# Mixture-of-experts items taken in pairs, with one fp32r gather for two items, and buffers laid out at multiples of 64 bytes

## What is computed

```python
def swiglu(x, w_gate, w_up, w_down):
    return (jax.nn.silu(x @ w_gate) * (x @ w_up)) @ w_down

def moe_swiglu(x, router_w, w_gate, w_up, w_down):      # N_EXPERTS 8, TOP_K 2, D_FF_EXPERT 3584
    logits = (x @ router_w).astype(jnp.float32)
    top_v, top_i = lax.top_k(logits, TOP_K)
    gates = jax.nn.softmax(top_v, axis=-1)
    combine = jnp.sum(jax.nn.one_hot(top_i, N_EXPERTS) * gates[..., None], axis=-2)
    y = jnp.zeros_like(x)
    for e in range(N_EXPERTS):
        y = y + combine[..., e:e + 1] * swiglu(x, w_gate[e], w_up[e], w_down[e])
    return y
```

## Time and profile before

| | us |
|---|---|
| median of 3 runs | 2152.03 (2149.94 to 2154.01) |
| the profiled execution, its own time | 2157.44 |
| its span, first to last instruction | 2154.8, granted TensorE clock 0.974 of full |
| attention, mixers, dense layer, router | 0 to about 1140 |
| items 0 to 7 and the last norm | about 1140 to 2154.8 |
| busy: PE, DVE, ACT | 2088.3 (97%), 1510.5 (70%), 1006.0 (47%) |

### The profile page before, as it was taken

How to read it: one execution, slowest core, us unless ns; L and a number is a source line. 1 busy time by engine, 2 the same in 40 slices (tenths; PEclk the granted TensorE clock), 3 DMA queues, 4 the chain that set the end, 5 groups by cost and what they waited for, 6 DMA issues and landing times.

```text
span 2154.8 us, 28044 instructions
## 1 busy us (share of the span) xinstructions
PE 2088.3 (97%) x10596; PEld 1665.9 (77%) x10596; DVE 1510.5 (70%) x1837; ACT 1006.0 (47%) x1082; POOL 50.9 (2%) x56
## 2 busy tenths in 40 slices
PE   7999999999998999999889999999999999999996
PEld 4786677756876799888747888888888888888885
DVE  4565434554597445438848888898888889888887
ACT  1121312122133334313236777777777777677674
POOL 0000000000011000000200000000000000000000
PEclk9998999999999999999988999999999999999999
DMA  9844043611621265452127999999999999999990
GB/s 356 279 140 159 30 146 99 226 43 38 217 79 40 92 202 196 172 183 81 44 107 291 395 355 368 347 355 372 330 374 337 367 346 355 376 327 375 333 368 20
DMA packets 238710, 502.18 MB, mean 233 GB/s; under 512 B 11275, under 2 KB 53027, under 8 KB 238627
## 3 DMA queue, kind: packets, MB, share of 16 engines
q1 hardware_dynamic: 238626, 501.03, 65.0%
HBM read 499.96 MB, written 1.05 MB: 233 GB/s over the span
## 4 chain that ended last, share of the span: by engine, by line
PE 89%; DVE 7%; ACT 2%; issue 1%; DMA 0%; SPq 0%; DVEq 0%; ACTq 0%
PE bank L1506 12%; PE bank L1489 9%; PE bank L1491 9%; PE bank L1490 9%; PE bank L757 6%; PE bank L1196 6%; PE bank L989 3%; PE bank L1064 3%; PE bank L765 3%; PE bank L1166 3%; PE bank L1433 3%; PE bank L1172 2%; PE bank L1404 2%; PE bank L1403 2%; PE bank L1402 2%; PE bank L1368 2%
## 5 line engine op out<-in xcount | busy, mean ns | idle before, releaser
L2650 DVE TENSOR_TENSOR ring_r<-ring,his 128x2048 fp32r<-128x2048 f32 x240 | 548.7, 2290 | 77.9 <-ACT his L1619 77.2
L1619 ACT ACTIVATE his<-ring 128x2048 fp32r<-128x2048 f32 x240 | 460.2, 1918 | 127.5 <-PE bank L1491 74.7
L1489 PE MATMUL bank<-his,xe_hi 128*128 128x512 f32 x896 | 354.1, 395 | 0.2 <-DVE ring_r L2650 0.2
L1491 PE MATMUL bank<-his,xe_lo 128*128 128x512 f32 x896 | 349.5, 390 | 0.0
L1490 PE MATMUL bank<-ring_r,xe_hi 128*128 128x512 f32 x704 | 274.2, 389 | 0.0
L2650 DVE TENSOR_TENSOR more_raw_r<-more_raw,his 128x2048 fp32r<-128x2048 f32 x96 | 219.7, 2290 | 27.5 <-ACT his L1619 27.4
L1619 ACT ACTIVATE his<-more_raw 128x2048 fp32r<-128x2048 f32 x96 | 184.2, 1919 | 54.6 <-PE bank L1506 29.1
L1489 PEld LDWEIGHTS bank<-his,xe_hi 128*128 128x128 f32 x896 | 168.2, 188 | 37.0 <-DVE ring_r L2650 3.3
L1491 PEld LDWEIGHTS bank<-his,xe_lo 128*128 128x128 f32 x896 | 168.2, 188 | 35.9
L1490 PEld LDWEIGHTS bank<-ring_r,xe_hi 128*128 128x128 f32 x704 | 132.3, 188 | 26.7
L1196 PE MATMUL bank<-uT,ring 128*128 128x256 f32 (+1 forms) x768 | 149.1, 356 | 0.0
(11 more groups left out here) (439 smaller groups left out, 3093.4 us busy)
## 6 DMA issues: line engine op xcount, KB each, us to landing
ring<-in_moe_w_gate_dram SPq DMA_DIRECT2D x96, 1024.0 KB, 5.2
ring<-in_moe_w_up_dram SPq DMA_DIRECT2D x80, 1024.0 KB, 5.3
ring<-in_moe_w_down_dram SPq DMA_DIRECT2D x64, 1024.0 KB, 4.9
more_raw<-in_moe_w_down_dram SPq DMA_DIRECT2D x48, 1024.0 KB, 5.0
ring<-in_w_in_dram SPq DMA_DIRECT2D x16, 2048.0 KB, 11.4
more_raw<-in_moe_w_up_dram SPq DMA_DIRECT2D x32, 1024.0 KB, 5.2
ring<-in_w_ada_dram SPq DMA_DIRECT2D x12, 2048.0 KB, 10.8
ring<-in_w_out_dram SPq DMA_DIRECT2D x8, 2048.0 KB, 9.6
```

The lines of the kernel that those rows point to most:

```text
L1489: mm(bank[b][:, :], xe_hi[:, k, :], hi[:, kk, :], start=(k == 0), stop=False)
L1491: last = mm(bank[b][:, :], xe_lo[:, k, :], hi[:, kk, :], start=False, stop=(k == KD - 1))
L1619: return go(out, in_, ACT.Copy, scale=scale)
L2650: tt(piece_lo(s), piece_raw(s), piece_hi(s).bitcast(fp32), ALU.subtract).then_inc(S("lo_ready"), 1)
```

## The change

Items are taken two at a time. The loop runs over pairs (`Fori(0, more) as m`, `more` is 3 here), its body holds the 14 chunks of items n = 2m and 2m + 1 (a = 0, 1), and an expert list of odd length is filled up with an empty item. x is split once into fp32r x_hi (ACT, two copies [128, 1024]) and x_lo (DVE, two subtractions, written over x); so total = ALPHA * x is formed before the router instead of after the first chunks. `pick` holds two items' places, 256 columns. A gather for a pair is 4 parts f of (4 matmuls from x_hi into bank 5, 4 from x_lo into bank 4), 256 columns each, fp32r; ACT copies all high parts and the odd low parts, DVE the even low parts. In the chunk j == 5 of the second item of a pair the parts stand between the down pieces and the first gate pieces. In the first item's chunk j == 5 nothing is gathered. The last norm's weights are loaded at the end, since they share memory with xe_lo. Buffers whose size is not a multiple of 64 bytes get a 32-byte filler behind them.

```diff
@@ memory
         def sb(name, shape, dtype=fp32):
-            return place[0].enter_context(nc.sbuf_tensor(name, shape, dtype))
+            made = place[0].enter_context(nc.sbuf_tensor(name, shape, dtype))
+            if name not in ("lnst", "lnmv") and 0 < math.prod(shape[1:]) * 4 % LINE <= LINE // 2:
+                place[0].enter_context(nc.sbuf_tensor(f"{name}_fill", [P, LINE // 8], fp32))
+            return made
@@ PE
-            def gather(half):
+            def gather(m, f, lo, b):
-                for f in range(4):
+                if f and not lo:
+                    pe.wait_ge(S("xe_hi_ready"), m * 4 + f)
+                elif f:
+                    pe.wait_ge(S("xe_lo_even" if f % 2 else "xe_lo_odd"), m * 2 + (f + 1) // 2)
+                src = x_lo if lo else x_hi
+                for kk in range(2):
+                    k = 2 * f + kk
                     for i in range(NT):
-                        last = mm(bank[5 - half][:, f * P:(f + 1) * P], x[:, i, (4 * half + f) * P:(4 * half + f + 1) * P],
-                                  pick[:, i, :], start=(i == 0), stop=(i == NT - 1))
+                        last = mm(bank[b][:, kk * 2 * P:(kk + 1) * 2 * P], src[:, i, k * P:(k + 1) * P], pick[:, i, :],
+                                  start=(i == 0), stop=(i == NT - 1))
...
+            def first_up(n, a, m, s0, b):
                 for half in range(2):
+                    if half:
+                        gather_both(m, 3)
+                    pe.wait_ge(S("xe_hi_ready"), m * 4 + (2 * half + 2))
+                    pe.wait_ge(S("xe_lo_even"), m * 2 + (half + 1))
+                    pe.wait_ge(S("xe_lo_odd"), m * 2 + (half + 1))
+                    up_piece(n, a, s0 + half, half, b)
...
                 if j == 5:
                     turn_hidden(g - 1)
+                if j == 5 and a == 1:
                     pe.wait_ge(S("picks_copied"), n + 1)
-                    pe.wait_ge(S("picked"), n + 2)
-                    gather(0)
+                    pe.wait_ge(S("picked"), m + 2)
+                    gather(m + 1, 0, False, 5)
                     pe.wait_ge(S("he_ready"), g)
-                    gather(1)
+                    gather(m + 1, 0, True, 4)
+                    down_piece(n, s0)
+                    gather_both(m + 1, 1)
+                    down_piece(n, s0 + 1)
+                    gather_both(m + 1, 2)
+                    first_up(n, to, m + 1, s0 + 2, b)
+                    s0 += 2
+                elif j == 5:
                     down_pieces(n, g - 1, s0)
                     s0 += 2
-                if j == 5:
-                    pe.wait_ge(S("xe_ready"), n * 2 + 4)
-                up_pieces(n, s0, b)
+                    up_pieces(n, to, s0, b)
@@ ACT
+                def gathered_hi(m, f, b):
+                    act.wait_ge(S("gathered_hi"), m * 4 + (f + 1))
+                    copy(xe_hi[:, :, 2 * f:2 * f + 2, :], bank[b][:, :].rearrange("p (k a s) -> p a k s", k=2, a=2))\
+                        .then_inc(S("xe_hi_ready"), 1)
+                    if f % 2:
+                        act.wait_ge(S("gathered_lo"), m * 4 + (f + 1))
+                        copy(xe_lo[:, :, 2 * f:2 * f + 2, :], bank[b - 1][:, :].rearrange("p (k a s) -> p a k s", k=2, a=2))\
+                            .then_inc(S("xe_lo_odd"), 1)
...
                         if j == 5 and r == 4:
                             copy_out(n)
+                        if j == 5 and a == 1 and r in (1, 2, 3, 4):
+                            gathered_hi(m + 1, r - 1, 5)
@@ DVE, experts(), ahead of the router's logits
+                for i in range(NT):
+                    for c in range(2):
+                        ts(total[:, i, cs], x[:, i, cs], ALPHA, None, ALU.mult).then_inc(S("acc_added"), 1)
+                for i in range(NT):
+                    dve.wait_ge(S("x_hi_ready"), i + 1)
+                    dve.wait_ge(S("acc_added"), 2 * i + 2)
+                    tt(x_lo[:, i, :], x[:, i, :], x_hi[:, i, :].bitcast(fp32), ALU.subtract).then_inc(S("x_lo_ready"), 1)
...
-                gathered_lo(0, [0])
-                combine()
-                gathered_lo(0, [1])
-                chunk(0, -2)
+                for f in (0, 2):
+                    gathered_lo(0, f, 4 + 2 * (f % 2))
+                chunk(0, 0, -2)
+                combine()
                 list_items()
```

More of the change, by code:

```diff
@@ L61 @@
 KE = D_FE // P
+LINE = 64
 RING = 5
@@ L136, in constants @@
     later["level0"] = lv[:, 0].T.copy()
+    later["tri_le"] = (row <= col).astype(np.float32)
+    later["tri_lt"] = (row < col).astype(np.float32)
+    later["iota"] = np.broadcast_to(r[None, :], (P, P)).astype(np.float32)
+    parts["fill"] = np.zeros((P, -sum(v.shape[1] for v in parts.values()) % 64), np.float32)
     at = {}
@@ new lines, in gather_both, with down_piece @@
+            def gather_both(m, f):
+                gather(m, f, False, 5)
+                gather(m, f, True, 4)
+            def down_piece(n, s):
+                half, q = piece_of(s)[3], piece_of(s)[2]
+                pe.wait_ge(S("lo_ready"), n * NPIECE + (s + 1))
+                hi, lo = piece_hi(s), piece_lo(s)
+                for kk in range(2):
+                    k = 2 * half + kk
+                    for a, w in ((he_hi, hi), (he_hi, lo), (he_lo, hi)):
+                        for c in range(2):
+                            last = mm(bank[6 + c][:, :], a[:, k, :], w[:, kk, 512 * c:512 * c + 512],
+                                      start=(q == 0 and k == 0 and a is he_hi and w is hi),
+                                      stop=(q == NQ - 1 and k == 3 and a is he_lo))
+                last.then_inc(S("piece_used"), 1)
@@ L1494, in down_pieces @@
             def down_pieces(n, g, s0):
                 pe.wait_ge(S("he_ready"), g + 1)
[L1497 to L1504, removed]
-                            for c in range(2):
-                                last = mm(bank[6 + c][:, :], a[:, k, :], w[:, kk, 512 * c:512 * c + 512],
-                                          start=(q == 0 and k == 0 and a is he_hi and w is hi),
-                                          stop=(q == NQ - 1 and k == 3 and a is he_lo))
-                    last.then_inc(S("piece_used"), 1)
+                down_piece(n, s0)
@@ L2679, in experts @@
                 for i in range(NT):
[L2680 removed]
+                    for a in range(2):
+                        last = ts(pick[:, i, a * P:(a + 1) * P], C("iota"), places[:, i, a:a + 1], None, ALU.is_equal)
                 last.then_inc(S("first_pick"), 1)
```

243 lines of the change are left out of this document (137 added, 106 removed).

## The result

The changed kernel takes 2181.18 us (median of 4 runs, 2177.92 to 2183.24), the kernel before 2153.02 (4 runs, 2149.94 to 2155.51): a ratio of 1.0124, 95% interval 1.011 to 1.0139. It is slower by 28 us between the medians (27 by the ratio), where 8.7 were forecast with a range up to 2168. The profiled execution took 2177.92 us, its span is 2176.1, against 2157.44 and 2154.8.

The account below looks back on a forecast made before the run. PE was taken to bound the kernel. First items −6.0, second items +7.5, prologue +5.5 and clock +1.7 summed to +8.7 us: 2166.1 on the profiled execution, 2160.7 on the median, range 2148 to 2168.

Parts of the forecast that it names:

- alignment: Term for the addresses of buffers that PE streams in the items: already at multiples of 64, taken as 0.
- (d): Rival: alignment pays over the first 1140 us, making the kernel faster; 2138 us at 2%; chance .08.
- Loop bookkeeping halves, on engines that wait for PE: Term for the expert loop's bookkeeping, listed among the rest at nothing.
- First items: End of each pair's first item: gather gone, down pieces earlier, PE idle 2.0 us; 4 × −1.5 = −6.0 us.
- the 0.3 that was given back for a late VectorE: In first items, 0.3 us off the −1.81 gain, for VectorE catching up behind ye_lo on the next chunk's low half.
- Second items: End of a pair's second item, three in the loop: new PE waits around the gather parts; 3 × 2.5 = +7.5 us.
- the wait at the second gate piece: In second items, PE waits 1.1 us there because ScalarE's copy_out delays the copies of gather part 3.
- Prologue: Router to first expert matmul and piece 4's low half: +3.3 and some 2.2 us of waiting; sum +5.5 us.
- the six operations: VectorE ahead of the first logits: four of total, two subtractions, 3.9 us; less 2.11 idle, logits copy 1.9 us later.
- Clock: PE's clock falls behind one of four new two-microsecond gaps in first items: +1.7 us, bounds 0 and 6.8.
- One sign of being wrong: A first 1120 us that changes by over 2 us would show the prediction wrong.
- the 15.3 us of gather work: PE work saved in the items: seven gathers of 3.83 us become three of 3.8.

Follow-up runs that it names:

- e1: The kernel before with the 32-byte fillers alone; 2160.1 us against 2155.01, ratio 1.0028.
- e2: The changed kernel without the 32-byte fillers; 2180.5 us, ratio 1.0125 against the kernel before.
- e8: The kernel before with PE's loop body two items long, work and addresses unchanged; 2162.49 us, ratio 1.004.
- e5: The changed kernel with 192 more bytes ahead of the experts' buffers, all seven alike modulo 256; 2170.17 us, ratio 1.0074 against the kernel before.
- e9: e5 with four edits of order (he_lo earlier, gather part 3 ahead of copy-out, x_lo and combine moved); 2166.35 us, ratio 1.0059 against the kernel before.
- e3: The changed kernel with 64 more bytes ahead of the experts' buffers; 2179.03 us.
- e10: e9 with the last chunk of a pair's first item in the usual order and its copy-out one chunk later; 2159.24 us, ratio 1.0026 against the kernel before.
- e7: The kernel before with 64 more bytes between his and xe_hi; 2177.05 us (one run).

## Why the prediction was wrong

**The step that failed is the one on alignment**: "The buffers that PE streams in the items (ring, his, xe, he) lie at multiples of 64 already ... I take 0." It asked which buffers the fillers bring to a multiple of 64, and overlooked that they move the others, which were alike modulo 256, apart. The two equal rows it rested on the earlier trace rows are fp32 matmuls of 128 columns at 275 ns, a form that says nothing of 512-column fp32r ones. The term was 0 and measured +17 us in the changed kernel. The fillers are not its only source: alone they cost the kernel before 7.9 us in the items (e1), and without them the changed kernel is as slow (e2), since its other buffers, xe_lo among them, had moved as well. The prediction looked at no address of the changed kernel. The rival drawn from the same edit, (d), had the other sign.

**The second missing term is the fetch.** "Loop bookkeeping halves, on engines that wait for PE" looked at the count of jumps, not at the length of the body. It measured +7.6 us for two jumps; e8 shows it alone, +7.3 between the medians. The trace of before could have told: no instruction packet in its loop, one every 25 us outside.

*First items*: right in place, a little too small. 1.90 us idle for 2.0 forecast, and a gain of 1.76 each where −1.5 stood: the 0.3 that was given back for a late VectorE did not come. *Second items*: right in place and size, +2.6 for +2.5. In e5, where matmuls have their old spacing, two items take 253.4 us from down pieces to down pieces, 4.8 more than before; less the jump's 3.8 that is 1.0 a pair, and 2.5 − 1.5 = 1.0 was forecast. The reason that I gave for the wait at the second gate piece (ScalarE in the copy-out) was wrong: e9 took the copy-out away from there and the wait stayed. *Prologue*: right within a microsecond, 3.1 + 1.8 for 3.3 + 2.2 (the six operations less the idle time are 1.8 us by the rows, where 1.9 was written). *Clock*: the kind was right, two falls where one was forecast; the other profiles of pairs with those gaps (e2, e3, e5, e9) have two, one, none and none behind them. One fall was a guess between none and four, and it could have come out either way. By the Trainium skill's rule (TensorE: Matmul & The Clock Gate, Why this matters for your kernels) there should have been none, since no gap came near its length; the windows at 1515 show one behind 1.90 us idle.

So the sum of what the prediction had named was right: +8.7 forecast, and the same terms measured 1.8 + 3.1 + 3.1 − 7.0 + 7.8 = +8.8. That they agree to 0.1 is luck in part, since one more fall (+1.4) and the second items (+0.3) are made up for by the first items (−1.0) and the prologue (−0.6). The range failed because it was built from bounds on known terms. One sign of being wrong was set too tight: the first 1120 us were to stay within 2 us, and they scatter by 8 between the profiles of kernels that share them.

Of the 15.3 us of gather work that the change takes from PE 7.0 arrive in first items; the rest of their gather had covered the wait for he_lo, which e10 avoids by another order (7 us). The second items take 7.8 back through their new waits, and the doubled body and the slower matmuls come on top.

## What to carry to other kernels

When a change to memory moves buffers, compare the start of what TensorE streams with the start of what it loads as stationary, modulo 256 bytes, before and after, and keep them alike; here 64 bytes raised the matmuls' spacing by up to 2.6%. When a loop's body grows, look whether the instruction queue is silent in the loop now; if it is, doubling the body can bring back the fetch, and here it brought 2.7 to 5.5 us of stalls at each jump. Work taken from the bounding engine is worth only what its waits leave of it, so price the wait that it covered first.

## What the runs showed of the hardware

- Start to start of 512-column fp32r matmuls depends on the relation of the addresses of streamed and stationary operand: 227.4 ns alike modulo 256, 229.6 to 233.3 ns else, in steady patterns that repeat in each item to a nanosecond (for long stretches in e3 236, 235, 234, 224, 232, 226; in e7 231, 236). In e7 it is the same with no load under way (233.4) and with VectorE and ScalarE idle (234.0). Why it is so, and whether 256 is the exact period, was not tried further.
- A loop whose PE body is one item (504 matmuls of 512 columns and their weight loads, above all; 1213 PE records in the trace) is fetched once. With two items (2364 to 2426 records) it is fetched in each turn, in 16 KB packets, and PE stands 2.7 to 5.5 us per jump. Where between the two lengths this begins, no run shows.
- The clock fell to 0.50 behind idle stretches of PE of 1.90 us (1515 us in the changed kernel) and behind the jumps' stalls in four profiles, and it did not behind two others of the changed kernel's four gaps of that kind.
- The first 1120 us, the same in the kernel before and the seven kernels made from it but for shifts, fillers and the length of PE's loop, scatter by 8 us between their profiles, with 72 to 85 us of them at the lower clock.
